# A state-space layer's convolution: the first tap moves from VectorE to ScalarE, and the silu behind it comes one block later

## What is computed

```
z, xbc, dt = jnp.split(h @ w_in, [SSM_INNER, SSM_INNER + SSM_CONV_DIM], axis=-1)
xbc = lax.conv_general_dilated(
    xbc, conv_w[:, None, :], window_strides=(1,), padding=((SSM_CONV - 1, 0),),
    dimension_numbers=('NWC', 'WIO', 'NWC'), feature_group_count=SSM_CONV_DIM) + conv_b
xbc = jax.nn.silu(xbc)
```

## Time and profile before

| | |
|---|---|
| median of 3 runs | 3108.59 us (3104.44 to 3113.85) |
| profiled execution | 3112.86 us, its span 3111.0 us |
| TensorE busy, granted clock | 2752.4 us (88%), 0.913 |
| VectorE, ScalarE, GpSimd busy | 1968.1, 1237.7, 1422.2 us |
| xbc's taps on VectorE | start from 1485.9 to 1585.3 us from the span's start |

### The profile page before, as it was taken

How to read it: one execution, slowest core, us unless ns; L and a number is a source line. 1 busy time by engine, 2 the same in 40 slices (tenths; PEclk the granted TensorE clock), 3 DMA queues, 4 the chain that set the end, 5 groups by cost and what they waited for, 6 DMA issues and landing times.

```text
span 3111.0 us, 49422 instructions
## 1 busy us (share of the span) xinstructions
PE 2752.4 (88%) x20583; PEld 2600.7 (84%) x20583; DVE 1968.1 (63%) x2280; ACT 1237.7 (40%) x1358; POOL 1422.2 (46%) x1126
## 2 busy tenths in 40 slices
PE   3998789999976999999789999999779979779797
PEld 3998679999965999998764999999669968468797
DVE  5657766676658666656766765766765454754553
ACT  2444444444444444434232444444444334334342
POOL 0890949579293692984730098494550000000000
PEclk7998989999987999999865999999889989789898
DMA  7765558667462675866620486675535535033452
GB/s 267 267 245 161 190 176 267 214 226 265 162 238 82 214 269 178 266 241 200 207 83 1 160 273 236 211 262 203 187 108 178 187 133 175 24 99 131 139 177 108
DMA packets 357173, 576.21 MB, mean 185 GB/s; under 512 B 22255, under 2 KB 297898, under 8 KB 356906
## 3 DMA queue, kind: packets, MB, share of 16 engines
q1 hardware_dynamic: 357034, 574.29, 54.2%
HBM read 573.20 MB, written 1.05 MB: 185 GB/s over the span
## 4 chain that ended last, share of the span: by engine, by line
PE 71%; DVE 13%; POOL 5%; ACT 4%; issue 4%; DMA 3%; SPq 1%; POOLq 0%; DVEq 0%; ACTq 0%
PE ps L1663 59%; PE ps L1716 3%; POOL mod_acc L647 3%; ACT whi L674 2%; PE ps L1722 1%; PE ps L2051 1%; POOL mod_w L642 1%; DVE wlo L1040 1%; DMA raw<-in_ffn_w_in_dram 1%; PE ps L2042 1%; DVE conv L1479 1%; PE ps L1773 1%; DVE z L1201 1%; DVE z L1179 1%; DMA raw<-in_ssm_w_in_dram 1%
## 5 line engine op out<-in xcount | busy, mean ns | idle before, releaser
L1040 DVE TENSOR_TENSOR wlo<-raw,whi 128x2048 fp32r<-128x2048 f32 x387 | 978.6, 2532 | 657.0 <-ACT whi L674 655.6
L1663 PE MATMUL ps<-H_hi,whi 128*128 128x256 f32 x3840 | 1099.4, 286 | 60.2 <-DVE conv L1479 21.8
L1663 PE MATMUL ps<-H_lo,whi 128*128 128x256 f32 x3840 | 1094.4, 285 | 0.0
L1663 PE MATMUL ps<-H_hi,wlo 128*128 128x256 f32 x3840 | 1094.0, 285 | 0.0
L674 ACT ACTIVATE whi<-raw 128x2048 fp32r<-128x2048 f32 (+1 forms) x402 | 759.9, 1892 | 645.6 <-DMA raw<-in_ffn_w_in_dram 259.7
L1663 PEld LDWEIGHTS ps<-H_hi,whi 128*128 128x128 f32 x3840 | 745.3, 194 | 68.6 <-issue 40.9
L647 POOL TENSOR_TENSOR mod_acc<-mod_acc,mod_w 128x512 f32<-128x512 f32 x450 | 793.0, 1788 | 0.0
L1663 PEld LDWEIGHTS ps<-H_lo,whi 128*128 128x128 f32 x3840 | 745.5, 194 | 0.2
L1663 PEld LDWEIGHTS ps<-H_hi,wlo 128*128 128x128 f32 x3840 | 745.1, 194 | 0.0
L1663 PE MATMUL ps<-A_hi,whi 128*128 (+1 forms) x1880 | 537.1, 286 | 21.0 <-DVE wlo L1040 21.0
L1663 PE MATMUL ps<-A_hi,wlo 128*128 (+1 forms) x1880 | 534.9, 285 | 0.0
(11 more groups left out here) (318 smaller groups left out, 2777.2 us busy)
## 6 DMA issues: line engine op xcount, KB each, us to landing
raw<-in_ffn_w_in_dram SPq DMA_DIRECT2D x176, 1024.0 KB, 5.3
mod_w<-in_w_mod_dram SPq DMA_DIRECT2D x180, 768.0 KB, 5.3
raw<-in_ffn_w_out_dram SPq DMA_DIRECT2D x88, 1024.0 KB, 4.8
raw<-in_w_gate_up_dram SPq DMA_DIRECT2D x22, 1024.0 KB, 5.1
raw<-in_ssm_w_in_dram SPq DMA_DIRECT2D x20, 1024.0 KB, 6.9
raw<-in_w_in_dram SPq DMA_DIRECT2D x14, 1024.0 KB, 5.1
raw<-in_diff_w_in_dram SPq DMA_DIRECT2D x12, 1024.0 KB, 7.7
raw<-in_w_down_dram SPq DMA_DIRECT2D x11, 1024.0 KB, 4.8
```

The source lines that it names most:

```text
L1040: tt(wlo[b % RAW][:, r], raw[b % RAW][:, r], whi[b % RAW][:, r].bitcast(F32), ALU.subtract).then_inc(w_lo, 1)
L1663: m = pe.matmul(out, l, r, start=first and i == 0, stop=last and i == 2, skip_group_check=rest)
```

## The change

ScalarE makes the tap of delay 0 with its bias out of PSUM (one instruction for each half c: scale and bias are pointers to a column of `V`) and signals it with a new semaphore `tap`. VectorE adds the other three taps, and waits for `tap` instead of `products` and `conv_out`. ScalarE's turn j becomes `convert(j + 2)`, silu(j - 1), tap(j), with silu(11) behind the loop.

```
-                for j in range(g.n):
-                    p = g.p + j
-                    convert(g.b + j + 2)
-                    act.wait_ge(banks_free[p % 2], plan.free_val[p])
+
+                def tap(j):
+                    act.wait_ge(products, g.l + (j + 1) * g.upb)
+                    if j >= 2:
+                        act.wait_ge(s["conv_out"], n["conv_out"] + j - 1)
+                    for c in range(2):
+                        nc.scalar.activation(conv[:, j % 2, c, :], ps[:, bank(g.p + j) + c, 0:S], ACT.Identity,
+                                             bias=vcol(column("ssm_conv_b", 2 * j + c)), scale=vcol(CONVW + 72 + 2 * j + c)).then_inc(s["tap"], 1)
+
+                def conv_silu(j):
+                    act.wait_ge(banks_free[(g.p + j) % 2], plan.free_val[g.p + j])
                     dst = XC[:, 2 * j:2 * j + 2, :] if j < 8 else (Bm if j < 10 else Cm)[:, 2 * (j % 2):2 * (j % 2) + 2, :]
                     nc.scalar.activation(dst, conv[:, j % 2], ACT.Silu).then_inc(s["conv_out"], 1)
+
+                for j in range(g.n):
+                    convert(g.b + j + 2)
+                    if j:
+                        conv_silu(j - 1)
+                    tap(j)
+                conv_silu(g.n - 1)
...
-                    dve.wait_ge(products, g.l + (j + 1) * g.upb)
-                    if j >= 2:
-                        dve.wait_ge(s["conv_out"], n["conv_out"] + j - 1)
-                    for d in range(4):
+                    for d in range(1, 4):
                         for c in range(2):
+                            if d == 1:
+                                dve.wait_ge(s["tap"], n["tap"] + 2 * j + c + 1)
                             src, dst = ps[:, bank(p) + c, 0:S - d], conv[:, j % 2, c, d:S]
                             w = vcol(CONVW + 24 * (3 - d) + 2 * j + c)
-                            if d == 0:
-                                i = ts(dst, src, w, vcol(column("ssm_conv_b", 2 * j + c)), ALU.mult, ALU.add)
-                            else:
-                                i = stt(dst, src, w, dst, ALU.mult, ALU.add)
+                            i = stt(dst, src, w, dst, ALU.mult, ALU.add)
```

More of the change, by code:

```diff
@@ L172 @@
     "diff": dict(fin_sq=4, fin_sum=4, fin_std=4, fin_n=4, fin_hi=4, fin_lo=4, **{k: 8 for k in ATT}),
-    "ssm": dict(conv_out=12, x_turned=8, x_out=8, dt_in=1, dt_ln=1, adt=1, acum=1, acum_t=1, cb=4, cb_out=4, spread=SSM_H,
+    "ssm": dict(tap=24, conv_out=12, x_turned=8, x_out=8, dt_in=1, dt_ln=1, adt=1, acum=1, acum_t=1, cb=4, cb_out=4, spread=SSM_H,
                 dec=SSM_H, dec_exp=SSM_H, mixing=SSM_H, ssd=SSM_H, y_out=SSM_H // 2,
@@ L1484, in dve_ssm @@
                                 i.then_inc(dve_step, 1)
-                                if d or c:
+                                if d > 1 or c:
                                     dve.wait_ge(dve_step, step[0] - 1)
```

## The result

The changed kernel takes **3092.2 us**, median of 9 runs (3084.2 to 3098.7); the kernel before took 3108.6 in the same series (9 runs, 3101.4 to 3120.1). The ratio is 0.9944, 95% interval 0.9930 to 0.9958: a gain of 13 to 22 us. The profiled execution has a span of 3090.4 us.

A forecast was written before the change was run, and what follows sets the result against it. Bound: ScalarE and VectorE waiting in turn, 8.03 us a block. Last silu from 1586.45 to 1557.6, gain 28.8, less 1.8 for long `wlo`: 27 us off 3112.86 is 3085.9, for the median 3082; range 3074 to 3092.

The forecast's parts named there:

- The ring and its end: Convolution row: ScalarE and VectorE wait for each other, 8.03 us a turn; the later silu leaves TensorE's 5.79 a block.
- The price of the tap: First tap on ScalarE, out of PSUM with two pointers: 555 ns, 1.03 us for two in a row, hidden.
- GpSimd's chain: End of the convolution row: the output row's first load waits for GpSimd's unit 11, so the last silu ends at 1557.6.
- Unit 5 ends at 1488.33: Start of the sum over GpSimd's modulation units: six units and nine full `wlo` from there end at 1542.4.
- rival A: Convolution row: TensorE alone bounds, feeding never shows; gain 31 to 35 us, 3074 to 3078; 13%.
- C: Nothing measurable, gain under 9.3 us: loads hold TensorE 2.1 us every turn, or the ring is no bound; 3% for both.
- The tail: From unit 11's end to the last silu: two loads 7.2 us, `whi` 1.9, `wlo` 2.29 and 0.8, taps 2.4, silu 0.63.
- The 1.8 us set aside for a long `wlo`: Convolution row: 1.8 us taken off the 28.8 us gain for a `wlo` kept out for long, leaving 27.
- What follows hangs on that silu: Behind the convolution row: `whi`, two tables, dt and copies XT follow the last silu through ScalarE's queue, only shifted.
- this sign of being wrong: The stretch from the last silu to the decay loop would be longer than before.
- The step from the traced execution to the median: Whole kernel: the profiled execution lay 4.3 us over the median, so 3085.9 became 3082 for the median.
- rival B: Convolution row: feeding of weights bites more, 6.3 us idle; gain 17 us, anything from 11 to 22, 3092; 24%.

The follow-up runs named there:

- run 2: Kernel before with only the silu put one block later, all four taps staying on VectorE: 3088.0 us, ratio 0.9921; measured again 3087.7 us, ratio 0.9933.
- run 3: Kernel before with only the first tap moved to ScalarE, the silu at its old place: 3105.1 us, ratio 0.9972.
- run 8: Changed kernel with each of ScalarE's 24 first taps issued twice, the extra one into an unused area: 3096.5 us, ratio 0.9956.
- Run 6: Changed kernel with GpSimd's last three modulation units (13 to 15) put behind index 24 of the weight order: 3092.4 us, ratio 0.9943.
- Run 12: Kernel of run 2 with GpSimd's modulation units from unit 2 on one index later in the weight order: 3083.7 us, ratio 0.9916.
- run 7: Kernel of run 2 with GpSimd's last three modulation units put behind index 24 of the weight order: 3089.4 us, ratio 0.9929.

## Why the prediction was right, and where it was not

**The ring and its end: right.** TensorE's pace of 5.79 us was measured as 5.78, its wait for taps as 0.4 us (forecast under 5). The order alone does it (run 2); the tap alone does not (run 3).

**The price of the tap: right.** 555 ns was worked out from one and no pointer; 547 to 568 were measured, a pair 1.02 us. The Trainium skill, ScalarE: Activation LUTs (What ACT_TABLE_LOAD costs), gives by its sum an estimate of 585, 5% more than the trace. It is hidden too, as doubling it showed: about 1 us of 13.5 came through (run 8). The rule on the same page of the Trainium skill (Rules for kernel authors), multiply and add on VectorE, would with that price have had the edit lose 1.1 us. In the conv row the order alone is 3.6 us shorter than both edits, so the trace agrees in the sign; but not by the difference of the two prices, for doubled taps cost the row about 1 us. What makes the 3.6 us is the end of the row: GpSimd reaches the end of unit 11 2 us later in the change (SP's issue at 1546.71, at 1544.69 with the order alone), and the change's first `wlo` of the output row begins at 1556.65 and takes 4.16 us with the last taps behind it; in the order alone that `wlo` takes 2.3.

**GpSimd's chain: right, and it decides in two of the three traces.** From the end of unit 5 to the end of unit 11 the prediction had 6 x 5.92 + 9 x 2.06 = 54.1 us; the chain shows 1546.69 - 1492.72 = 54.0. In the third trace unit 11 ended 2 us sooner after the last `Z`, and `wlo` of 4.24, 3.81 and 5.62 us in the last turns made the same 78.3 us. Run 6 confirms it from the other side: without the last three units the silu comes 3.3 us sooner.

**The term that was mis-sized is its start, "Unit 5 ends at 1488.33".** It was read off one execution as if the change left it alone. It came at 1492.72, 4.4 us later: 1.5 us because everything ahead of the first `Z` ended later in this execution, 2.9 in the z row. There, in all three traces of the change, one of unit 0's multiplications fell behind a `wlo`; GpSimd and SP in the changed kernel:

```profile
1448.26 4.06 POOL L638 TENSOR_SCALAR mod_acc<-mod_w,cond 128x512 f32<-128x512 f32 x3
...
1452.35 0.34 SPq L589 DMA_DIRECT2D mod_w<-in_w_mod_dram  x1
1452.73 0.43 SPq L582 DMA_DIRECT2D raw<-in_ssm_w_in_dram  x1
```

and before:

```profile
1445.74 2.02 POOL L638 TENSOR_SCALAR mod_acc<-mod_w,cond 128x512 f32<-128x512 f32 x3
...
1447.79 0.34 SPq L589 DMA_DIRECT2D mod_w<-in_w_mod_dram  x1
```

4.06 us against 2.02, and the unit itself begins 2.5 us later (its `pool_tick` at 1446.17 and 1443.65). So SP, which waits for unit 0, issues the weights of the z row 4.6 us later. TensorE then waits 4.5 us for `wlo`, and behind that wait its clock is low:

```profile
1464.97 0.55 PE L1673 MATMUL ps<-H_hi,whi 128*128 128x256 f32 x1 [4.51 <-DVE wlo L1054]
...
1469.80 0.41 PE L1673 MATMUL ps<-H_lo,whi 128*128 128x256 f32 x1
```

From 1464.9 to 1470.0 the matmuls start every 0.21 us instead of every 0.12, at a granted clock of 0.50. Before, the same wait was

```profile
PE ps L1663 <- DVE wlo L1040: 1.7, 1, 1.7
```

and the clock stayed at 1.00. The prediction overlooked this wait: the stretch that it cites as a row without a gap, for rival A and against C, begins just behind it, at 1460.60. For TensorE the z row, from the first `Z` to the end of block 0, grew from 42.9 to 48.1 us. With the 1.5 us ahead of the first `Z` that is why it left the conv row at 1554.3 and not at 1547.55, although the row itself ran nearly without a pause.

Run 12 shows the cause of the gap: with the load ahead of SP's wait it is gone, although the multiplications take 4.07 us there too. Whether the changed order *makes* them fall so is open. Kernels with it show a z row of 42.5 or 42.6 (six times), 40.2, 39.0 and 39.1, the kernel before 39.0, 40.2 and 40.7. But the tap alone, which has the old order, shows 42.4, and nothing that was edited runs before this point.

**The tail was 1.9 us longer than its terms**: SP's issue and the two loads 8.0 for 7.2, `whi` 1.92, the last `wlo` 4.16 for 3.1. With 4.4 - 0.1 + 1.9 this makes 1557.6 into the 1563.8 of the trace. The 1.8 us set aside for a long `wlo` nearly cover this.

**"What follows hangs on that silu" missed 2.3 us.** The part behind is 195.6 us in all three traces of the change and 193.3 to 193.5 in those of before; with the order alone 192.4. It is not simply the tap's: runs 3 and 8 have the tap and 193.8 and 193.7. The stretch from the last silu to the first `dec` of the decay loop is no longer than before (21.2 and 21.3 us), so this sign of being wrong did not show; the 2.3 us arise in the loop and behind it. I did not settle by what.

**The step from the traced execution to the median was wrong.** It lay 4.3 us over the median of the kernel before, and I took these 4.3 us off the changed kernel too, from 3085.9 to 3082. But it was slow in the conv row, 6.3 us longer than in the two other traces, and the change removes just this. Nothing was left to take off. Without this step the forecast is 3085.9. The last silu came 4.4 us after the 1559.4 that a gain of 27 us means, the part behind took 2.3 more, and the rest of the program 0.4 less: together the 3092.2 measured. As a gain over the other traces the 27 us would have been 27 - 6.3 = 20.7, within the measured 13 to 22.

**Which case it was.** The time lies at the very end of the range (3092.2 against 3092), outside the 3077 to 3086 that I held likeliest, and by size it is rival B (17 us), to which I gave 24%, not the forecast of 23 to 31. By its mechanism it is the forecast, with B's kind of wait at one place only, in the z row; inside the conv row TensorE was idle 0.4 us, not B's 6.3. Of the marks that were to show each step, the last silu (1563.8, not 1555 to 1560) and "all after 1600 only shifted" failed. ScalarE's wait for VectorE's taps did not nearly vanish either: it fell from 77.8 us (the silus into `XC`, `Bm` and `Cm`) to 13.1, and what it waits for most is not TensorE (5.7 us) but the weights (17.6). `wlo` stayed under 4 us in all but one turn.

## What to carry to other kernels

When two engines wait for each other in turn, look first at the order of the work on either: moving one instruction behind the next block's work took the whole ring away (21 to 25 us), while moving work between the engines took 9 and, on top of the order, nothing that these runs show. When the ring is gone, the next bound here is an engine that looked harmless, GpSimd, through a load that waits for it in a shared DMA queue: count its units from a fixed point before asking what TensorE could do. And take two or three traces of the kernel before: a stage in which two engines shut each other out can differ by 6 us between two executions, more than most terms of such a sum.

## What the runs showed of the hardware

- VectorE's `wlo` and GpSimd's work shut each other out, and the price depends on who is inside: `wlo` took 2.3 us alone, and 2.9 to 4.2, 4.78, 5.6, 5.85, 6.56 and 8.05 when it met GpSimd; GpSimd's three multiplications took 2.03 alone and 4.06 with one `wlo` among them. VectorE's delayed taps out of PSUM took 459 to 486 ns in all of this.
- The two fell into step for four turns in runs 7 and 12, with turns of nearly the same length (7.95 and 7.98 us in run 12), and then each turn had the collision. In run 7 this came in blocks where the moved units don't run; what differed there was the phase of the two at the start of the stage.
- Blocks of 48 matmuls ran at 5.78 us each and clock 1.00 through 65 us with one pause of 0.4 us. In the ring before, with nine waits of up to 5.9 us, the granted clock fell to the lower level again and again (0.85 over the stretch, 0.90 now with the dt product and what follows it in the stretch). In the z row it was 0.50 for 5.1 us behind a wait of 4.5 us, and stayed at 1.00 behind one of 1.7.
